# The second input projection's first group multiplies X without its norm, in a float32 kernel of a hybrid layer pair

## The chip, the cores and the metric

The kernel runs on one core of a Trainium2 chip. The time is the device time of one execution in microseconds; the median of three runs is given. The engines are named as in the profile: PE (TensorE), DVE (VectorE), ACT (ScalarE), POOL (GpSimd) and SP (SyncE, which here issues DMAs).

## What is computed

256 tokens of width 2048 pass two layers. The first is attention and a state space scan, then a gated feed-forward of width 5632. The second begins with a norm that is modulated by a vector `c`, and multiplies it by a weight matrix of 7168 columns:

```python
mod = c_act @ w_ada + b_ada
shift, scale, gate = jnp.split(mod, 3, axis=-1)
h = rms_norm_2(x, g) * (1.0 + scale[:, None]) + shift[:, None]
proj = jnp.einsum('bsd,df->bsf', h, w_in)
q_a, k_a, v_a, z_a, q_r, k_r, v_r, z_r = jnp.split(proj, IN_SPLIT_IDX, axis=-1)
```

with `rms_norm_2(x, g) = x * rsqrt(mean(x * x) + 1e-6) * g`. Attention and retention over these, gated by silu of `z_a` and `z_r`, an output projection, the residual and a last norm follow. All is float32. Since the root of the norm is one number per token, `h @ w_in` is also `r * ((x * g * (1 + scale)) @ w_in) + shift @ w_in`.

## The kernel before

X is held transposed: 16 tiles of 128 features x 256 tokens. Each weight matrix comes as a stream of units of 128 x 1024 (two 128-row tiles of 512 columns each). SP loads a unit to one of eight `raw` slots. ACT rounds it to `whi` (line 326, `split`), DVE puts the rest in `wlo` (line 692, `split`); both have four slots. An activation tile is held as `gh` and `gl` in the same way. PE multiplies each unit by three products, hi x hi, hi x lo, lo x hi: 24 matmuls of 256 columns. Eight units make a group of 512 output features, in two PSUM banks; groups use banks 0 and 1, and 2 and 3, in turn. ACT's split of unit n waits until PE has used unit n - 4; DVE's waits for ACT's. Each engine's program is written out in order, with semaphores between them; nothing is reordered.

At the border, the last block of the feed-forward (`B_IN2 - 1`) is eight units. Its last two (`last_pair`, lines 1400 to 1404) finish the last four X tiles one at a time in banks 4 to 7 (`own`); DVE adds them to X (`last_add`, line 1172). ACT squares X in chunks of four tiles (`squares`, lines 341 and 345), DVE sums the squares, and PE reduces them to a column (`column_squares`, line 1421). ACT takes the root (line 361), DVE its reciprocal (line 1200), and PE spreads it over 128 partitions (line 1433). Then, for each of the 16 tiles t:

```python
TH = X[t] * modT[16 + t] * spread        # DVE, line 1206
gh[t] = round(TH + modT[t])              # ACT, line 612
gl[t] = (TH + modT[t]) - gh[t]           # DVE, line 1211
```

`modT` holds shift in columns 0 to 15 and gain x (1 + scale) in 16 to 31. Both loops carry a split behind the tiles 3, 5, 7, ... 15 (`TURNS`). PE's slots n (`stream_in`, n counts the units of this projection) wait in group 0 for each tile's `gl` (`ready`). Group 0 (columns of `z_a`, QB tiles 0 to 3) starts with `product_high_first` (line 1364). ACT copies a finished group to `QB` (line 656). `idle` (line 1455) is a matmul whose result nobody reads. POOL only issues DMAs, the last at 1035.49 us.

## Time and profile before

| | us |
|---|---|
| median of 3 runs (1539.02 to 1539.16) | 1539.11 |
| the profiled execution | 1538.62 |
| its span, first to last instruction | 1536.9 |
| PE busy | 1527.4 (99%) |
| DVE busy | 1135.7 (74%) |
| ACT busy | 780.8 (51%) |
| POOL busy | 27.3 (2%) |

The mean granted clock of PE is 0.999. A busy PE can still be slow, since overlapping matmuls count as busy whatever their spacing. So the distance between the starts of matmuls is to be read beside the busy share. Times below are from the span's start.

### The profile page before, as it was taken

Reading aid. Unit: us, or ns where it says so; the run is one execution under the profiler, and the core shown is the slowest. Engines: PE = TensorE matmul, PEld = TensorE weight load, DVE = VectorE, ACT = ScalarE, POOL = GpSimd, SP = SyncE. Lnnn points to the kernel's source line nnn. Section 1 sums busy time; section 2 is a strip of 40 time slices with the busy share of each in tenths; the row PEclk is TensorE's granted clock in tenths of the full one; section 3 lists DMA queues with packets and bytes.
Section 4 is the critical chain, followed back from the end, with each engine's and each line's share of the span. In section 5 each row is a group of like instructions: output and inputs, shape, how many; then the busy total and the mean of one; then the engine's idle time right before and its main releaser. Section 6 shows DMA issues by size and latency. Waiting matters only on the chain. (4 is left out here: it accounts for less than half of the span.)

```text
span 1536.9 us, 32122 instructions
## 1 busy us (share of the span) xinstructions
PE 1527.4 (99%) x12610; PEld 1486.9 (97%) x12610; DVE 1135.7 (74%) x1371; ACT 780.8 (51%) x933; POOL 27.3 (2%) x55
## 2 busy tenths in 40 slices
PE   9999999999999999999999999999999999999998
PEld 8999997999999999999999999999999989999998
DVE  7877777657987878788788887879854644764754
ACT  7545455545554444444444444445554643454554
POOL 0000000000000000000000000000000000000000
PEclk9999999999999999999999999999999999999999
DMA  9574556457877767677686776866475555445451
GB/s 352 169 272 165 193 178 219 150 166 274 306 281 249 286 233 273 244 251 273 235 292 230 263 272 221 300 220 216 151 247 193 197 192 161 162 157 187 153 184 62
DMA packets 86029, 339.25 MB, mean 221 GB/s; under 512 B 9648, under 2 KB 9920, under 8 KB 79424
## 3 DMA queue, kind: packets, MB, share of 16 engines
q1 hardware_dynamic: 77856, 281.05, 52.8%
q0 software_dynamic: 7232, 54.55, 10.0%
q10 hardware_dynamic: 864, 2.53, 0.4%
q8 instruction: 59, 0.97, 0.2%
q14 instruction: 18, 0.15, 0.0%
HBM read 335.97 MB, written 2.12 MB: 220 GB/s over the span
## 5 line engine op out<-in xcount | busy, mean ns | idle before, releaser
L692 DVE TENSOR_TENSOR wlo<-raw,whi 128x1024 fp32r<-128x1024 f32 x528 | 643.3, 1223 | 346.7 <-ACT whi L326 343.0
L326 ACT ACTIVATE whi<-raw 128x1024 fp32r<-128x1024 f32 x528 | 557.6, 1059 | 647.5 <-PE PS L1333 574.6
L1329 PE MATMUL PS<-gh,whi 128*128 128x256 f32 x3096 | 864.0, 279 | 0.4 <-DVE gl L1211 0.3
L1331 PE MATMUL PS<-gl,whi 128*128 128x256 f32 x3096 | 856.5, 277 | 0.0
L1333 PE MATMUL PS<-gh,wlo 128*128 128x256 f32 x3096 | 856.5, 277 | 0.0
L1329 PEld LDWEIGHTS PS<-gh,whi 128*128 128x128 f32 x3096 | 582.0, 188 | 5.3 <-issue 2.6
L1331 PEld LDWEIGHTS PS<-gl,whi 128*128 128x128 f32 x3096 | 581.7, 188 | 0.8
L1333 PEld LDWEIGHTS PS<-gh,wlo 128*128 128x128 f32 x3096 | 581.5, 188 | 0.0
L1329 PE MATMUL PS<-ah,whi 128*128 128x256 f32 x688 | 189.9, 276 | 0.0
L1331 PE MATMUL PS<-al,whi 128*128 128x256 f32 x688 | 189.9, 276 | 0.0
L1333 PE MATMUL PS<-ah,wlo 128*128 128x256 f32 x688 | 189.9, 276 | 0.0
L1331 PEld LDWEIGHTS PS<-al,whi 128*128 128x128 f32 x688 | 129.2, 188 | 0.0
L1333 PEld LDWEIGHTS PS<-ah,wlo 128*128 128x128 f32 x688 | 129.2, 188 | 0.0
L1329 PEld LDWEIGHTS PS<-ah,whi 128*128 128x128 f32 x688 | 129.1, 188 | 0.0
L1117 DVE SCALAR_TENSOR_TENSOR ada_w<-ada_w,c_act 128x2048 f32<-128x2048 f32 x40 | 91.4, 2285 | 0.0
L1375 PE MATMUL PS<-whi,gh 128*128 128x512 f32 x192 | 76.8, 400 | 0.0
L1378 PE MATMUL PS<-wlo,gh 128*128 128x512 f32 x192 | 75.5, 393 | 0.0
L1377 PE MATMUL PS<-whi,gl 128*128 128x512 f32 x192 | 75.3, 392 | 0.0
L708 DVE TENSOR_TENSOR X<-PS,X 128x1024 f32<-128x1024 f32 x47 | 57.2, 1218 | 0.0
L1375 PEld LDWEIGHTS PS<-whi,gh 128*128 128x128 f32 x192 | 36.1, 188 | 8.6 <-issue 0.8
L1377 PEld LDWEIGHTS PS<-whi,gl 128*128 128x128 f32 x192 | 36.1, 188 | 7.8
L1378 PEld LDWEIGHTS PS<-wlo,gh 128*128 128x128 f32 x192 | 36.1, 188 | 7.5
(259 smaller groups left out, 899.6 us busy)
## 6 DMA issues: line engine op xcount, KB each, us to landing
raw<-weights SPq DMA_DIRECT2D x528, 512.0 KB, 3.6
ada_w<-w_ada POOLq DMA_DIRECT2D x48, 1024.0 KB, 6.4
...
```

Of the source, the lines that this page charges most:

```text
L326: act.activation(whi[:, j % SPLIT, :], raw[:, j, :], ACT.Copy).then_inc(s_hi, 1)
L692: dve.tensor_tensor(wlo[:, j % SPLIT, :], raw[:, j, :], whi[:, j % SPLIT, :].bitcast(F32), ALU.subtract).then_inc(s_lo, 1)
L708: dve.tensor_tensor(x, acc_tiles(par), x, ALU.add).then_inc(s_evac, 1)
L1117: dve.scalar_tensor_tensor(w, w, 1.0, c_act[:, :], ALU.mult, ALU.mult, accum_out=modT[:, bass.ds(i * ADA_STEP + (ADA_FIRST - ADA_STEP + k) ...
L1329: pe.matmul(out[:, t, :], whi[:, b, w], hi[:, kt, :], start=first and half == 0 and (apart or t % 2 == 0), stop=False, skip_group_check=True)
L1331: pe.matmul(out[:, t, :], whi[:, b, w], lo[:, kt, :], start=False, stop=False, skip_group_check=True)
L1333: mm = pe.matmul(out[:, t, :], wlo[:, b, w], hi[:, kt, :], start=False, stop=last and half == 1, skip_group_check=True)
L1375: pe.matmul(out, gh[:, kt, m], whi[:, b, w], start=first and half == 0, stop=False, skip_group_check=True)
L1377: pe.matmul(out, gl[:, kt, m], whi[:, b, w], start=False, stop=False, skip_group_check=True)
L1378: mm = pe.matmul(out, gh[:, kt, m], wlo[:, b, w], start=False, stop=last and half == 1, skip_group_check=True)
```

## The change

Group 0 of the second input projection no longer waits for the norm. ACT and DVE form `YH` and `YL`, the two parts of X x gain x (1 + scale), with no root. Each has two more columns in which the shift stands, so that one matmul of 258 columns gives both products. Group 0 goes to banks 4, 5, 6 and 3, one output tile each (`deferred`). The squares of chunks 1 and 2 are added on POOL, those of the last four tiles (`NEAR`) on DVE. PE sums them over partitions in one matmul in slot 1, into bank 0. ACT takes the root of 256 columns in slot 2, DVE the reciprocal in slot 3 (`rb`). In slot 7 DVE evacuates group 0 times `rb`, and copies the shift's column to `zbias`, which becomes the bias of the silu in slot 16.

`TH`, `gh` and `gl` for the groups from 1 on are made in slots 3 to 14, by the table `TURNED_IN`, which says how many tiles a slot makes. ACT and DVE now split one unit in every slot, with units 2 and 3 ahead of slot 0. `idle` in slot 6, the column form of this root and its spreading are gone.

```diff
+TURNED_IN = (0, 0, 0, 2, 1, 2, 1, 2, 1, 2, 1, 2, 1, 1)
...
+        deferred = (PS[:, 4, 0:S + 2], PS[:, 5, 0:S + 2], PS[:, 6, 0:S + 2], PS[:, 3, 0:S + 2])
+        zbias = small[:, 234:238]
+        def turns(n):
+            done = [sum(TURNED_IN[:m + 1]) for m in range(len(TURNED_IN))]
+            return range(done[n] - TURNED_IN[n], done[n]) if n < len(TURNED_IN) else range(0)
...
+            for c in (1, 2):
+                pool.wait_ge(s_sq, SQUARES[2] + c + 1)
+                if c > 1:
+                    pool.wait_ge(s_sum, SUMS[2] + 1)
+                pool.tensor_tensor(SQX2[:, 0, :, :], SQX2[:, 0, :, :], SQX2[:, 1, :, :], ALU.add).then_inc(s_sum, 1)
+            pool.wait_ge(s_sum, SUMS[2] + 2)
+            pool.tensor_tensor(SQX2[:, 0, 0:2, :], SQX2[:, 0, 0:2, :], SQX2[:, 0, 2:4, :], ALU.add).then_inc(s_far, 1)
+            pool.wait_ge(s_far, 1)
+            pool.tensor_tensor(SQX2[:, 0, 0, :], SQX2[:, 0, 0, :], SQX2[:, 0, 1, :], ALU.add).then_inc(s_far, 1)
...
+            def unscaled_hi(first, end):
+                for t in range(first, end):
+                    act.activation(YH[:, t, 0:S], X[:, t, :], ACT.Copy, scale=modT[:, 16 + t:17 + t]).then_inc(s_yh, 1)
+            def turned_hi(t):
+                act.wait_ge(s_h, t + 1)
+                act.activation(gh[:, t, :], TH[:, t % 8, :], ACT.Identity, bias=modT[:, t:t + 1]).then_inc(s_gh, 1)
+            act.wait_ge(s_mt, 2)
+            act.activation(YH[:, :, S:S + 2], modT[:, 0:DT].unsqueeze(2).to_broadcast([P, DT, 2]), ACT.Copy).then_inc(s_yh, 1)
             for d in range(4):
                 if d < 2:
                     split(B_IN2 - 1, LEAD + 2 * d)
...
                 if d < 3:
                     act.wait_ge(s_evac, G_IN2 - 4 + d + 3)
                 squares(2, d, SQX2)
-                if d == 2:
-                    act.activation(small[:, 241:242], col("eps"), ACT.Sqrt).then_inc(s_warm, 1)
-            column_root(2)
-            for t in range(DT):
-                act.wait_ge(s_h, t + 1)
-                act.activation(gh[:, t, :], TH[:, t % 8, :], ACT.Identity, bias=modT[:, t:t + 1]).then_inc(s_gh, 1)
-                if t in TURNS:
-                    split(B_IN2 - 1, LEAD + 6 + TURNS.index(t))
-            act.dma_start(c2[:, :, :, :], const2).then_inc(s_c2, 16)
+                if d < 3:
+                    unscaled_hi(4 * d, 4 * d + 4)
+            split(B_IN2 - 1, LEAD + 6)
+            split(B_IN2 - 1, LEAD + 7)
+            unscaled_hi(12, DT)
...
             def slot2(n):
...
+                if n == 2:
+                    root(2, D)
+                for t in turns(n):
+                    turned_hi(t)
+                if n == len(TURNED_IN):
+                    act.dma_start(c2[:, :, :, :], const2).then_inc(s_c2, 16)
+                if n == 16:
+                    act.wait_ge(s_zb, 2)
+                    for t in range(4):
+                        ins = act.activation(QB[:, ZA2 + t, :], QB[:, ZA2 + t, :], ACT.Silu, bias=zbias[:, t:t + 1])
+                    ins.then_inc(s_zs, 1)
+                if n == 17:
+                    gate_silu(QB, ZA2 + 4, G_IN2 + 2 + 2, s_zs)
...
-                    split(B_IN2, LEAD + n)
-                if n % 8 == 7:
+                split(B_IN2, LEAD + n)
+                if n % 8 == 7 and n > 7:
                     g = n // 8
                     act.wait_ge(s_used, 8 * B_IN2 + n + 1 + SPLIT)
+                    if g == 1:
+                        act.wait_ge(s_evac, G_IN2 + 3)
                     act.activation(QB[:, 4 * g:4 * g + 4, :], acc_tiles((G_IN2 + g) % 2), ACT.Copy).then_inc(s_evac, 1)
...
+            def unscaled_lo(first, end):
...
                 add_to_x(8 * (B_IN2 - 1) + 2 * d + 1, G_IN2 - 4 + d, (G_IN2 - 4 + d) % 2, 4 * d)
+                if d == 0:
+                    dve.wait_ge(s_yh, 1)
+                    dve.wait_ge(s_mt, 2)
+                    dve.tensor_tensor(YL[:, :, S:S + 2], modT[:, 0:DT].unsqueeze(2).to_broadcast([P, DT, 2]),
+                                      YH[:, :, S:S + 2].bitcast(F32), ALU.subtract).then_inc(s_yl, 1)
             split(B_IN2 - 1, LEAD + 4)
-            sum_chunk(2, 1, SQX2)
+            unscaled_lo(0, 4)
             add_to_x(8 * (B_IN2 - 1) + 5, G_IN2 - 2, (G_IN2 - 2) % 2, 8)
-            fold(2, 1, SQX2)
             last_add(0)
-            dve.wait_ge(s_sq, SQUARES[2] + 3)
-            link(dve.tensor_tensor(SQX2[:, 1, 0:2, :], SQX2[:, 1, 0:2, :], SQX2[:, 1, 2:4, :], ALU.add))
+            split(B_IN2 - 1, LEAD + 5)
             last_add(1)
-            dve.tensor_tensor(SQX2[:, 1, 0, :], SQX2[:, 1, 0, :], SQX2[:, 1, 1, :], ALU.add).then_inc(s_dve, 1)
-            links[0] += 1
+            unscaled_lo(4, 5)
             last_add(2)
-            dve.wait_ge(s_dve, links[0])
-            dve.wait_ge(s_fold, 3)
-            dve.tensor_tensor(SQX2[:, 0, 0, :], SQX2[:, 0, 0, :], SQX2[:, 1, 0, :], ALU.add).then_inc(s_near, 1)
-            near(2, 0, SQX2, 1)
+            unscaled_lo(5, 6)
             last_add(3)
             dve.wait_ge(s_tile, 4)
             dve.sem_inc(s_evac, 1)
-            split(B_IN2 - 1, LEAD + 5)
-            dve.wait_ge(s_mt, 1)
-            dve.wait_ge(s_rcol, 1)
-            dve.reciprocal(rcol[:, 0, :], rcol[:, 0, :]).then_inc(s_icol, 1)
-            dve.wait_ge(s_spread, 1)
-            for t in range(DT + 1):
-                if t < DT:
-                    if t >= 8:
-                        dve.wait_ge(s_gl, 2 * DT + 10 + t - 7)
-                    dve.scalar_tensor_tensor(TH[:, t % 8, :], X[:, t, :], modT[:, 16 + t:17 + t], spread(2),
-                                             ALU.mult, ALU.mult).then_inc(s_h, 1)
-                if t:
-                    k = t - 1
-                    dve.wait_ge(s_gh, 2 * DT + 6 + k + 1)
-                    dve.scalar_tensor_tensor(gl[:, k, :], TH[:, k % 8, :], modT[:, k:k + 1], gh[:, k, :].bitcast(F32),
-                                             ALU.add, ALU.subtract).then_inc(s_gl, 1)
-                    if k in TURNS:
-                        split(B_IN2 - 1, LEAD + 6 + TURNS.index(k))
+            dve.wait_ge(s_sq, SQUARES[2] + 7)
+            link(dve.tensor_tensor(NEAR[:, 0:2, :], NEAR[:, 0:2, :], NEAR[:, 2:4, :], ALU.add))
+            link(dve.tensor_tensor(NEAR[:, 0, :], NEAR[:, 0, :], NEAR[:, 1, :], ALU.add))
+            dve.wait_ge(s_far, 2)
+            dve.tensor_tensor(SQX2[:, 0, 0, :], SQX2[:, 0, 0, :], NEAR[:, 0, :], ALU.add).then_inc(s_fold, 1)
+            split(B_IN2 - 1, LEAD + 6)
+            unscaled_lo(6, 8)
+            split(B_IN2 - 1, LEAD + 7)
+            def turned_tile(t):
+                if t >= 8:
+                    dve.wait_ge(s_gl, 2 * DT + 10 + t - 7)
+                dve.scalar_tensor_tensor(TH[:, t % 8, :], X[:, t, :], modT[:, 16 + t:17 + t], rb[:, :],
+                                         ALU.mult, ALU.mult).then_inc(s_h, 1)
+            def turned_lo(t):
+                dve.wait_ge(s_gh, 2 * DT + 6 + t + 1)
+                dve.scalar_tensor_tensor(gl[:, t, :], TH[:, t % 8, :], modT[:, t:t + 1], gh[:, t, :].bitcast(F32),
+                                         ALU.add, ALU.subtract).then_inc(s_gl, 1)
+            def turned_slot(n):
+                if n < 3:
+                    unscaled_lo((8, 10, 13)[n], (10, 13, 16)[n])
+                if n == 3:
+                    inverse_root(2)
+                    dve.wait_ge(s_rb, 3)
+                for t in turns(n):
+                    turned_tile(t)
+                    if t:
+                        turned_lo(t - 1)
+                if n == len(TURNED_IN):
+                    turned_lo(DT - 1)
+                if n == 7:
+                    finished(8 * B_IN2 + 7, G_IN2)
+                    gates = PS[:, 4:7, :]
+                    dve.tensor_tensor(QB[:, ZA2:ZA2 + 3, :], gates[:, :, 0:S], rb[:, :].unsqueeze(1).to_broadcast([P, 3, S]),
+                                      ALU.mult).then_inc(s_zb, 1)
+                    dve.tensor_copy(zbias[:, 0:3], gates[:, :, S])
+                    dve.tensor_copy(zbias[:, 3:4], deferred[3][:, S:S + 1])
+                    dve.tensor_tensor(QB[:, ZA2 + 3, :], deferred[3][:, 0:S], rb[:, :], ALU.mult).then_inc(s_zb, 1)
+                    dve.wait_ge(s_zb, 2)
+                    dve.sem_inc(s_evac, 1)
...
             for n in range(IN2_SLOTS):
-                if n >= len(TURNS) - 2:
-                    split(B_IN2, LEAD + n)
+                split(B_IN2, LEAD + n)
+                turned_slot(n)
                 slot2(n)
...
+            def product_deferred(b, u):
+                for kt in (2 * u, 2 * u + 1):
+                    pe.wait_ge(s_yl, kt + 2)
+                    for t in range(4):
+                        if u == 0 and kt == 0 and t < 3:
+                            pe.wait_ge(s_tile, t + 1)
+                        w = slice(512 * (kt % 2) + P * t, 512 * (kt % 2) + P * t + P)
+                        hi, lo = YH[:, kt, 0:S + 2], YL[:, kt, 0:S + 2]
+                        pe.matmul(deferred[t], whi[:, b, w], hi, start=(kt == 0), stop=False, skip_group_check=True)
+                        pe.matmul(deferred[t], whi[:, b, w], lo, start=False, stop=False, skip_group_check=True)
+                        mm = pe.matmul(deferred[t], wlo[:, b, w], hi, start=False, stop=(kt == DT - 1), skip_group_check=True)
                 mm.then_inc(s_used, 1)
...
-                if blk == B_IN2 and n == 0:
-                    product_high_first(acc_tiles(grp % 2), need)
+                if blk == B_IN2 and g == 0:
+                    product_deferred(n % SPLIT, u)
                     return
+                if blk == B_IN2 and n == 8:
+                    pe.wait_ge(s_root, 3)
                 product(n % SPLIT, acc_tiles((grp + g) % 2), (2 * u, 2 * u + 1), u == 0, u == 7, gh, gl,
-                        ready=need if g == 0 else None)
+                        ready=need if g == (1 if blk == B_IN2 else 0) else None)
...
-            column_squares(2, SQX2)
 
 
             def slot2(n):
-                if n == 6:
-                    idle(2)
+                if n == 1:
+                    sum_squares(2, SQX2)
```

ACT, from the root of the second layer's norm on, where `whi<-raw` is a split and `gh<-TH` a tile. Before:

```order
L361 ACTIVATE small<-PS,prm 128x2 [waits s_ss]
L612 ACTIVATE gh<-TH,modT 128x256 [waits s_h] x4
L326 ACTIVATE whi<-raw 128x1024 [waits s_used,s_raw2]
L612 ACTIVATE gh<-TH,modT 128x256 [waits s_h] x2
L326 ACTIVATE whi<-raw 128x1024 [waits s_used,s_raw3]
L612 ACTIVATE gh<-TH,modT 128x256 [waits s_h] x2
L326 ACTIVATE whi<-raw 128x1024 [waits s_used,s_raw4]
L612 ACTIVATE gh<-TH,modT 128x256 [waits s_h] x2
```

After:

```order
L344 ACTIVATE whi<-raw 128x1024 [waits s_used,s_raw6]
L372 ACT_TABLE_LOAD
L372 ACTIVATE rb<-PS,prm 128x256 [waits s_ss]
L344 ACTIVATE whi<-raw 128x1024 [waits s_used,s_raw7]
L621 ACTIVATE gh<-TH,modT 128x256 [waits s_h] x2
L344 ACTIVATE whi<-raw 128x1024 [waits s_used,s_raw0]
L621 ACTIVATE gh<-TH,modT 128x256 [waits s_h]
L344 ACTIVATE whi<-raw 128x1024 [waits s_used,s_raw1]
L621 ACTIVATE gh<-TH,modT 128x256 [waits s_h] x2
L344 ACTIVATE whi<-raw 128x1024 [waits s_used,s_raw2]
L621 ACTIVATE gh<-TH,modT 128x256 [waits s_h]
```

The splits stood behind two tiles each; now every slot begins with a split, with two tiles or one behind it.

DVE around the fold of the squares, in the changed kernel:

```order
L1241 TENSOR_TENSOR NEAR<-NEAR 128x512 [waits s_tile,s_sq]
L1242 TENSOR_TENSOR NEAR<-NEAR 128x256 [waits s_dve]
L1244 TENSOR_TENSOR SQX_85<-SQX_85,NEAR 128x256 [waits s_far,s_dve]
L728 TENSOR_TENSOR wlo<-raw,whi 128x1024 [waits s_hi]
L1208 SCALAR_TENSOR_TENSOR YL<-X,modT,YH 128x256 [waits s_yh] x2
L728 TENSOR_TENSOR wlo<-raw,whi 128x1024 [waits s_hi] x2
L1208 SCALAR_TENSOR_TENSOR YL<-X,modT,YH 128x256 [waits s_yh] x2
L728 TENSOR_TENSOR wlo<-raw,whi 128x1024 [waits s_hi]
L1208 SCALAR_TENSOR_TENSOR YL<-X,modT,YH 128x256 [waits s_yh] x3
L728 TENSOR_TENSOR wlo<-raw,whi 128x1024 [waits s_hi]
L1208 SCALAR_TENSOR_TENSOR YL<-X,modT,YH 128x256 [waits s_yh] x3
```

Six splits and ten `YL` tiles stand between the fold (the third row here) and the reciprocal. In the kernel before, DVE in group 0 ran `TH` and `gl` in turn, with a split behind two of each:

```order
L692 TENSOR_TENSOR wlo<-raw,whi 128x1024 [waits s_hi]
L1206 SCALAR_TENSOR_TENSOR TH<-X,modT,PS 128x256
L1211 SCALAR_TENSOR_TENSOR gl<-TH,modT,gh 128x256 [waits s_gh]
L1206 SCALAR_TENSOR_TENSOR TH<-X,modT,PS 128x256
L1211 SCALAR_TENSOR_TENSOR gl<-TH,modT,gh 128x256 [waits s_gh]
L692 TENSOR_TENSOR wlo<-raw,whi 128x1024 [waits s_hi]
L1206 SCALAR_TENSOR_TENSOR TH<-X,modT,PS 128x256
L1211 SCALAR_TENSOR_TENSOR gl<-TH,modT,gh 128x256 [waits s_gh]
```

DVE in slots 3 to 5 now:

```order
L728 TENSOR_TENSOR wlo<-raw,whi 128x1024 [waits s_hi]
L776 RECIPROCAL rb<-rb 128x256 [waits s_root]
L1253 SCALAR_TENSOR_TENSOR TH<-X,modT,rb 128x256 [waits s_rb]
L1253 SCALAR_TENSOR_TENSOR TH<-X,modT,rb 128x256
L1259 SCALAR_TENSOR_TENSOR gl<-TH,modT,gh 128x256 [waits s_gh]
L728 TENSOR_TENSOR wlo<-raw,whi 128x1024 [waits s_hi]
L1253 SCALAR_TENSOR_TENSOR TH<-X,modT,rb 128x256
L1259 SCALAR_TENSOR_TENSOR gl<-TH,modT,gh 128x256 [waits s_gh]
L728 TENSOR_TENSOR wlo<-raw,whi 128x1024 [waits s_hi]
L1253 SCALAR_TENSOR_TENSOR TH<-X,modT,rb 128x256
L1259 SCALAR_TENSOR_TENSOR gl<-TH,modT,gh 128x256 [waits s_gh]
L1253 SCALAR_TENSOR_TENSOR TH<-X,modT,rb 128x256
```

The reciprocal stands behind slot 3's split, and slots of two tiles and of one follow each other.

## Rows read from the trace of the kernel before

**Rows 1.** The page: busy time by engine; costliest groups (busy us, mean ns).
```profile
PE 1527.4 (99%) x12610; PEld 1486.9 (97%) x12610; DVE 1135.7 (74%) x1371; ACT 780.8 (51%) x933; POOL 27.3 (2%) x55
...
L692 DVE TENSOR_TENSOR wlo<-raw,whi 128x1024 fp32r<-128x1024 f32 x528 | 643.3, 1223 | 346.7 <-ACT whi L326 343.0
```

**Rows 2.** PE in order of time at the border (start us, us, line, operands, idle before).
```profile
1095.28 0.28 PE L1404 MATMUL PS<-ah,wlo 128*128 128x256 f32 x1
1095.39 1.02 PE L1421 MATMUL PS<-cst,CG 128*128 128x1 f32 x8
...
1098.26 0.71 PE L1433 MATMUL PS<-cst,small 128*128 128x128 f32 x4 [0.62 <-DVE small L1200]
1098.80 1.03 PE L1455 MATMUL PS<-cst 128*128 128x256 f32 x4
1100.17 0.36 PE L1364 MATMUL PS<-gh,whi 128*128 128x256 f32 x1 [0.34 <-ACT gh L612]
```

**Rows 3.** PE in order of time in groups 0 and 1.
```profile
1108.56 0.36 PE L1329 MATMUL PS<-gh,whi 128*128 128x256 f32 x1
...
1111.70 0.36 PE L1329 MATMUL PS<-gh,whi 128*128 128x256 f32 x1 [0.16 <-DVE gl L1211]
...
1120.81 1.02 PE L1455 MATMUL PS<-cst 128*128 128x256 f32 x4
...
1124.40 0.28 PE L1329 MATMUL PS<-gh,whi 128*128 128x256 f32 x1
...
1146.16 0.28 PE L1329 MATMUL PS<-gh,whi 128*128 128x256 f32 x1
```

**Rows 4.** DVE in order of time in group 0.
```profile
1099.01 0.87 DVE L1206 SCALAR_TENSOR_TENSOR TH<-X,modT,PS 128x256 f32<-128x256 f32 x2 [0.80 <-PE PS L1433]
...
1106.40 1.23 DVE L692 TENSOR_TENSOR wlo<-raw,whi 128x1024 fp32r<-128x1024 f32 x1 [0.35 <-ACT whi L326]
1107.55 0.47 DVE L1206 SCALAR_TENSOR_TENSOR TH<-X,modT,PS 128x256 f32<-128x256 f32 x1
1107.94 0.48 DVE L1211 SCALAR_TENSOR_TENSOR gl<-TH,modT,gh 128x256 fp32r<-128x256 f32 x1
...
1109.55 1.22 DVE L692 TENSOR_TENSOR wlo<-raw,whi 128x1024 fp32r<-128x1024 f32 x1 [0.34 <-ACT whi L326]
...
1111.08 0.48 DVE L1211 SCALAR_TENSOR_TENSOR gl<-TH,modT,gh 128x256 fp32r<-128x256 f32 x1
```

**Rows 5.** ACT in order of time, ahead of the border and in group 0.
```profile
1082.82 1.06 ACT L341 ACTIVATE SQX<-X 128x1024 f32<-128x1024 f32 x1 [2.43 <-DVE X L708]
1083.78 2.05 ACT L326 ACTIVATE whi<-raw 128x1024 fp32r<-128x1024 f32 x2
...
1093.20 1.28 ACT L607 ACT_TABLE_LOAD   x1
...
1105.33 1.05 ACT L326 ACTIVATE whi<-raw 128x1024 fp32r<-128x1024 f32 x1
...
1108.05 0.51 ACT L612 ACTIVATE gh<-TH,modT 128x256 fp32r<-128x256 f32 x1 [1.29 <-DVE TH L1206]
1108.47 1.04 ACT L326 ACTIVATE whi<-raw 128x1024 fp32r<-128x1024 f32 x1
```

**Rows 6.** DVE in order of time at the border: small adds.
```profile
1093.06 0.42 DVE L1172 TENSOR_TENSOR X<-PS,X 128x256 f32<-128x256 f32 x1
1093.39 0.68 DVE L1184 TENSOR_TENSOR SQX<-SQX 128x512 f32<-128x512 f32 x1
```

**Rows 7.** Groups of DVE by line and shape: the reciprocal of the root.
```profile
L739 DVE RECIPROCAL rb<-rb 128x256 f32<-128x256 f32 x2 | 3.5, 1750 | 0.6 <-ACT rb L356 0.6
```

**Rows 8.** Busy us of each engine in two stretches, then granted clock (PEclk).
```profile
1095.00:1101.00 6.00, 4.87 (x36) 4.27 (x36) 4.58 (x11) 2.26 (x8) 0.00 (x0) 1.00 0.27 89
1530.00:1537.00 7.00, 1.37 (x13) 1.13 (x11) 1.50 (x2) 1.72 (x3) 0.00 (x0) 0.77 0.80 300
```

**Rows 9.** Groups of POOL, the costliest (busy us, mean ns, idle before).
```profile
L308 POOL DMA_DIRECT2D ada_w<-w_ada x46 | 24.4, 530 | 757.1 <-DVE ada_w L1117 591.9 <-DVE ada_w L1026 165.3
```

More of the change, by code:

```diff
@@ L670, in _ @@
             column_root(3)
[L671 removed]
+            act.wait_ge(s_icol, 1)
             for b in range(4):
@@ L1492, in sum_squares @@
                     pe.wait_ge(s_root, k)
-                pe.matmul(PS[:, 4, 0:S], ones, buf[:, 0, 0, :], start=True, stop=True).then_inc(s_ss, 1)
+                pe.matmul(PS[:, 0 if k == 2 else 4, 0:S], ones, buf[:, 0, 0, :], start=True, stop=True).then_inc(s_ss, 1)
             pe.wait_ge(s_zero, 1)
```

83 lines of the change are left out of this document (32 added, 51 removed).

## The prediction

> **What bounds the kernel now.** First the page: TensorE (PE) is busy 1527.4 of 1536.9 us [rows 1], so only its holes and the spacing of its matmuls can be changed. Then PE in order of time around the border from the first block to the second. Matmuls follow each other every 0.1133 us, 24 of them a unit (one 1024-column piece of weights), 2.72 us. At 1095.39 that stops: column sums, a wait for the root's reciprocal at 1098.26, two idle matmuls, and the first product of the second input projection only at 1100.17 [rows 2], 4.78 us later. Inside group 0 the units come too slowly: one at 1108.56, the next at 1111.70 with a wait for gl, 3.14 us on, and an idle pair of matmuls stands at 1120.81 [rows 3]; group 0 ends at 1124.40 instead of 1100.17 + 8 x 2.72 = 1121.93, 2.47 us. So the border costs 4.78 + 2.47 = 7.25 us over bare products, and group 1 runs from 1124.40 to 1146.16, 21.76 us, without any loss [rows 3].
>
> Third, who sets the pace inside group 0. VectorE (DVE) and ScalarE (ACT) go in a ring: DVE's low half of a weight piece at 1106.40, tile TH at 1107.55, ACT's gh of it at 1108.05, ACT's next high half whi at 1108.47, DVE's next low half at 1109.55 [rows 4, 5]. That is 3.15 us round (3.14 in the other rounds), for two X tiles a round, against PE's 2.72. This ring is what the change spreads out, and where I look.
>
> **The change part by part.** *Removed.* The 4.78 us hole goes: group 0 multiplies YH and YL, which need no root. Group 0 also loses its ring waits and idle pair, 2.47 us. Added on PE: 192 matmuls of 258 instead of 256 columns (192 x 0.1133 x 2/256 = 0.17 us); one sum of squares of the same form as an idle matmul (about half of the 1.03 us of two [rows 2], 0.5 us); and a wait for X tiles 13 and 14 in the first unit. DVE adds them at about 1095.3 and 1096.1, with 0.42 us each [rows 6], since a split and a YL stand between; PE loses some 0.5 us. If PE were all, the sum would be -7.25 + 1.17 = -6.1 us.
>
> *What runs before the root is known.* Up to ACT's first square at 1082.82 [rows 5] nothing moves. Issue spacings from the rows: ACT 0.97 for a 1024-column piece (1082.82 to 1083.78 [rows 5]) and 0.42 for a 256-column tile (1108.05 to 1108.47 [rows 5]); DVE 1.14 for a split and 0.395 for a tile (1106.40 to 1107.55 to 1107.94 [rows 4]). ACT now puts four YH tiles behind each square: 1082.82 + 0.97 + 4 x 0.42 = 1085.4 for the split that came at 1083.78. DVE follows: splits at 1086.5 and 1087.7, add of chunk 1 at 1088.8, done 1090.05. ACT then: second square 1090.07, four YH, split at 1092.7; the third square waits for DVE's add of chunk 2 (behind a split and four YL, done 1093.9): 1093.93, four YH, four squares of the last chunk, done 1098.3. DVE adds these up (0.71 and 0.47), adds POOL's part, and the fold is issued at 1099.53. PE wants it at about 1101.5, after unit 1, so PE is not held here. But DVE stood about 1.1 us idle and has a backlog behind it.
>
> *The backlog.* From 1099.95 DVE issues six splits, ten YL tiles and the reciprocal of 256 columns (1.75 us [rows 7]): 6 x 1.14 + 10 x 0.395 + 1.78 = 12.57 us. Its inputs come in time (ACT's root with its table load, 1.28 us [rows 5], ends about 1107.8). The first TH tile starts at 1112.5, where before it was 1099.01 [rows 4]. That by itself is no loss: PE needs the first gl only at unit 8, some 1118.3.
>
> *The ring again, now the decisive term.* From slot 3 on, ACT does in each slot: whi of unit n+4, then gh of **all** the TH tiles of that slot; DVE does the low half, then TH, gl. So ACT's next whi waits for the slot's last TH. A slot of one tile is the round of before: 1.15 + 0.50 + 0.42 + 1.08 = 3.15 us. A slot of two adds one TH and one gl ahead of the second TH: 3.15 + 2 x 0.395 = 3.94 us. The table gives slots 4 to 13 one, two, one, two, one, two, one, two, one, one: six of 3.15 and four of 3.94 = 34.7 us, where PE would use 27.2. In slot 7 DVE also turns group 0 out (768 + 256 columns of PSUM and two copies, some 1.5 us; 0.27 of it not covered by the wait for ACT).
>
> Sum: TH of tile 0 at 1112.52; two TH, ACT's gh, then whi of slot 4 at 1113.86; + 34.7 + 0.3 = whi of slot 14 at 1148.9; + 1.09 (ACT's half) + 1.14 (DVE's half) + 0.48 (gl of tile 15) + 0.14 (to PE, as 1111.08 + 0.48 to 1111.70 [rows 3, 4]) = 1151.7. This gl stands in slot 14 behind a split that waits for unit 14, and PE needs it for the second half of unit 15, 1.36 us and a restart of 0.09: group 1 ends at **1153.1**. Before, it ended at 1146.16 [rows 3]. So +6.9 us: PE arrives at unit 8 about 6 us earlier and then loses some 12 us in front of the halves of units 10 to 15. What is late next: nothing; from unit 16 on the weights are four units ahead, and a unit of PE covers a split on ACT and DVE again (1.05 and 1.22 us [rows 4, 5]). The four silu of 256 instead of one of 1024, some 0.7 us more on ACT, lie under that.
>
> *POOL.* Two adds of 1024, one of 512 and one of 256 columns go to POOL, which shows no arithmetic in this trace, only DMA issues of 0.53 us [rows 9]. Bounds: as on DVE (1.22 [rows 1], 0.68 and 0.42 [rows 6]), or four times that, the ratio of DVE's slowest 256-column step to an add (1.75 to 0.42 [rows 6, 7]). Cover: POOL has from 1095.1 (third square) to 1099.5, 4.4 us, for 1.22 + 0.68 + 0.42 = 2.32 us of adds at DVE's pace, so up to 1.9 times it costs nothing; above that each microsecond goes one to one into the fold, then the backlog and the end (at four times +7). I take two and a half times, the middle: 2.5 x 2.32 = 5.8, with the third square 0.4 late, +1.8 us.
>
> Forecast: 1538.62 (the profiled execution) + 6.9 + 1.8 = 1547.3; the median of before is 0.49 above it, so **1547.8 us**.
>
> **A rule against the change.** No row of before has POOL and DVE adding at once. The Trainium skill (SBUF — State Buffer, Who interferes with whom) says that a VectorE instruction with two SBUF inputs contends with a GpSimd one that reads SBUF, and that the second to issue blocks fully until the first ends; no run here shows it. GPSIMD Engine Reference (Elementwise — side-by-side cycle accounting) has a GpSimd add at 1.96 times the VectorE's; by that price POOL would still be all but covered, and the forecast would be near 1546.2.
>
> **Rivals.**
> *The ports (35%).* DVE's splits and YL tiles have both inputs in SBUF. If a POOL add holds them up whole, the two large ones (2 x 3.05 us at my price) fall among DVE's work between 1091 and 1099.5, of which 1.1 us is idle: +5 on DVE, all of it ahead of the ring. 1552.8; with POOL as fast as DVE about 1549. This mechanism is the rule above.
> *Faster (4%).* The ring does not close: ACT issues the next whi without standing behind the slot's gh, so that a slot takes what DVE is busy, 1.14 + 0.79 or 1.14 + 1.58 us. DVE then catches up with PE after its late start at 1112.5, and only the gl of tiles 14 and 15, which stand behind splits that wait for units 13 and 14, hold PE, 1.8 us together. Group 1 ends at 1118.3 + 21.76 + 1.8 = 1141.8, 4.3 us early: 1534.8. The point from which it decides is the mean of the ten rounds: at 2.8 us the end is that of before (1113.9 + 28 + 2.85 + 1.4 = 1146.2), at my 3.5 it is 7 us later. For it: DVE's own work is short enough. Against it: the 3.15 us round of rows 4 and 5, in which ACT and DVE idle in turn, by order of issue, and the order listed in the change.
> *Nothing to measure (5%).* The mean round is 2.6 to 3.0 us: 1539.
>
> *The clock (4%).* PE will stand about 12 of 28 us. If the granted clock (1.00 with 4.87 of 6 us busy, 0.77 with 1.37 of 7 [rows 8]) falls to its lower level, 1.2 GHz, units take 5.44 us, longer than the ring's 3.5: six units x 1.9 = 11 more, 1559.
> *The change does not do what it says*, since group 0 waits for YL instead: YL comes at 0.395 a tile against 1.36 us of PE each, with a split per two; in the ports' case it can happen, and is in its price.
>
> **How the numbers follow.** Forecast case 51%, between 1546.0 (POOL covered) and 1553 (four times DVE's time). The ports 35%, clock 4%, faster 4%, nothing 5%, 1% unnamed. The range 1545.0 to 1553.5 takes the forecast case and most of the ports' and leaves under 2 in 10 out. A measurement of this kernel tells about 0.2%, 3.1 us, from no change; slower than that has 0.51 + 0.35 + 0.04 = 0.90 (with the unnamed 0.91), same 0.05, faster 0.04.
>
> **What the changed profile would show.** Right: products of 258 columns directly behind 1095.39 with gaps under 1 us in the first unit; the next unit 8 near 1118 to 1122; DVE's low halves spaced 3.15 and 3.94 us in turn from 1115 to 1149, with DVE idle for ACT and ACT idle for DVE; PE waiting for gl in both halves of units 10 to 15, 1.1 to 1.8 us each; then no waits. Wrong: spacing of 2.72 us there; DVE's splits or YL stretched beyond 1.22 and 0.48 us while POOL adds (ports); POOL's 1024 columns beyond 5 us; a granted clock under 0.95 between 1120 and 1155.

## The result

The changed kernel took 1555.28 us, median of four executions, beside 1539.13 us of the kernel before on the same chip: ratio 1.0098, 95% interval 1.0086 to 1.011. The forecast was 1547.8 with a range of 1545.0 to 1553.5, so the sign was right and the size outside the range. The four executions are 1555.53, 1555.03, 1556.04 and 1550.87. The lone one at 1550.87 matters: five more executions of the same kernel on another chip, told below, lie between 1550.69 and 1552.02. Two causes have to be kept apart: about 12 us that every execution has, and 4.3 us more in three of those first four. Five executions of three kernels below took some 26 us longer than the others of the same kernel (1561.71 to 1570.27), and they are left out of every median and ratio.

The profiled execution is the one of 1555.53 (span 1553.8). Its trace runs later than that of before even ahead of the border: a split of ACT there, released by PE in both, starts at 1080.20 instead of 1079.33. Against before, its times are therefore read less 0.9 us.

### The profile page after: what moved, and what is told of

Same layout as the page of the kernel before. It is cut to its first block, busy times and chain, and to the rows that moved or that the text cites. A ratio compares the mean times of both kernels' runs of the same rounds, so it can differ in the third digit from the quotient of the medians.

```text
span 1553.8 us, 32123 instructions
## 1 busy us (share of the span) xinstructions
PE 1533.3 (99%) x12584; PEld 1492.0 (96%) x12584; DVE 1146.4 (74%) x1388; ACT 787.0 (51%) x951; POOL 34.5 (2%) x59
## 4 chain that ended last, share of the span: by engine, by line
PE 91%; DVE 5%; ACT 2%; issue 1%; ACTq 0%; DVEq 0%
PE PS L1399 26%; PE PS L1401 26%; PE PS L1403 26%; PE PS L1447 3%; PE PS L1445 3%; PE PS L1448 3%; DVE wlo L728 2%; ACT whi L344 1%; PE PS L1601 1%; PE PS L1622 1%; DVE conv_acc L804 1%; PE PS L1790 0%; PE PS L1584 0%; DVE YL L1208 0%; DVE TH L1253 0%
## 5 line engine op out<-in xcount | busy, mean ns | idle before, releaser
L1399 PE MATMUL PS<-gh,whi 128*128 128x256 f32 x3040 | 850.1, 280 | 9.4 <-DVE gl L1259 9.4
L1401 PE MATMUL PS<-gl,whi 128*128 128x256 f32 x3040 | 842.6, 277 | 0.0
L1403 PE MATMUL PS<-gh,wlo 128*128 128x256 f32 x3040 | 842.5, 277 | 0.0
L1399 PEld LDWEIGHTS PS<-gh,whi 128*128 128x128 f32 x3040 | 571.6, 188 | 14.9 <-DVE gl L1259 6.2
L1403 PEld LDWEIGHTS PS<-gh,wlo 128*128 128x128 f32 x3040 | 572.0, 188 | 0.0
L1401 PEld LDWEIGHTS PS<-gl,whi 128*128 128x128 f32 x3040 | 571.1, 188 | 0.8
```

The lines of the kernel that those rows point to most:

```text
L1399: pe.matmul(out[:, t, :], whi[:, b, w], hi[:, kt, :], start=first and half == 0 and (apart or t % 2 == 0), stop=False, skip_group_check=True)
L1401: pe.matmul(out[:, t, :], whi[:, b, w], lo[:, kt, :], start=False, stop=False, skip_group_check=True)
L1403: mm = pe.matmul(out[:, t, :], wlo[:, b, w], hi[:, kt, :], start=False, stop=last and half == 1, skip_group_check=True)
```

## The profile after

The page, with the same rows as [rows 1] of before. PE's busy time rose by 5.9 us though it stands longer in front of `gl`, so its matmuls follow each other more slowly somewhere.

```profile
PE 1533.3 (99%) x12584; PEld 1492.0 (96%) x12584; DVE 1146.4 (74%) x1388; ACT 787.0 (51%) x951; POOL 34.5 (2%) x59
...
L728 DVE TENSOR_TENSOR wlo<-raw,whi 128x1024 fp32r<-128x1024 f32 x528 | 643.1, 1222 | 353.5 <-ACT whi L344 349.9
```

PE's waits between 1080 and 1180 us (waited for: us in total, times, longest). The column form's waits of [rows 2] are gone; 12.8 us of new ones stand there.

```profile
PE PS L1399 <- DVE gl L1259: 9.4, 8, 1.6
PE PS L1434 <- DVE X L1217: 3.4, 3, 1.8
```

**The ring.** DVE in order of time behind the root (start us, us, line, operands; in brackets the idle time before and who ended it). This answers [rows 4].

```profile
1117.10 1.75 DVE L776 RECIPROCAL rb<-rb 128x256 f32<-128x256 f32 x1
1118.88 0.88 DVE L1253 SCALAR_TENSOR_TENSOR TH<-X,modT,rb 128x256 f32<-128x256 f32 x2
...
1121.29 1.23 DVE L728 TENSOR_TENSOR wlo<-raw,whi 128x1024 fp32r<-128x1024 f32 x1 [0.87 <-ACT whi L344]
1122.44 0.48 DVE L1253 SCALAR_TENSOR_TENSOR TH<-X,modT,rb 128x256 f32<-128x256 f32 x1
1122.83 0.48 DVE L1259 SCALAR_TENSOR_TENSOR gl<-TH,modT,gh 128x256 fp32r<-128x256 f32 x1
1124.44 1.23 DVE L728 TENSOR_TENSOR wlo<-raw,whi 128x1024 fp32r<-128x1024 f32 x1 [1.13 <-ACT whi L344]
...
1128.38 1.23 DVE L728 TENSOR_TENSOR wlo<-raw,whi 128x1024 fp32r<-128x1024 f32 x1 [1.13 <-ACT whi L344]
...
1131.53 1.23 DVE L728 TENSOR_TENSOR wlo<-raw,whi 128x1024 fp32r<-128x1024 f32 x1 [1.13 <-ACT whi L344]
...
1156.30 1.23 DVE L728 TENSOR_TENSOR wlo<-raw,whi 128x1024 fp32r<-128x1024 f32 x1 [1.13 <-ACT whi L344]
```

The splits are 3.15, 3.94 and 3.15 us apart, and so on to 1156.30, with DVE idle 1.13 us for ACT each time. Only slot 7, where DVE also turns group 0 out, is longer, 4.30 us. Those are the forecast's two slots to the hundredth. ACT's side of the same ring, where it stands for DVE's `TH` and takes up the next `whi` only behind it, answers [rows 5]:

```profile
1151.66 0.51 ACT L621 ACTIVATE gh<-TH,modT 128x256 fp32r<-128x256 f32 x1 [1.69 <-DVE TH L1253]
1152.08 1.05 ACT L344 ACTIVATE whi<-raw 128x1024 fp32r<-128x1024 f32 x1
1154.81 0.51 ACT L621 ACTIVATE gh<-TH,modT 128x256 fp32r<-128x256 f32 x1 [1.69 <-DVE TH L1253]
...
1155.22 1.04 ACT L344 ACTIVATE whi<-raw 128x1024 fp32r<-128x1024 f32 x1
```

PE in order of time where the ring holds it: the last four of its eight waits for `gl` (in units 13, 14 and 15, the last in both halves), then the first product of group 2. This answers [rows 3].

```profile
1148.14 0.38 PE L1399 MATMUL PS<-gh,whi 128*128 128x256 f32 x1 [1.43 <-DVE gl L1259]
...
1152.08 0.39 PE L1399 MATMUL PS<-gh,whi 128*128 128x256 f32 x1 [0.95 <-DVE gl L1259]
...
1155.32 0.36 PE L1399 MATMUL PS<-gh,whi 128*128 128x256 f32 x1 [1.59 <-DVE gl L1259]
...
1157.97 0.39 PE L1399 MATMUL PS<-gh,whi 128*128 128x256 f32 x1 [1.03 <-DVE gl L1259]
...
1159.49 0.28 PE L1399 MATMUL PS<-gh,whi 128*128 128x256 f32 x1
```

Less the 0.9 us, group 1 ends at 1158.6, 12.4 us after the 1146.16 of [rows 3]; the forecast had 6.9 without POOL and 8.7 with it.

**POOL and DVE.** POOL in order of time, all its arithmetic, and DVE beside it.

```profile
1092.01 2.61 POOL L323 TENSOR_TENSOR SQX<-SQX 128x1024 f32<-128x1024 f32 x1 [55.10 <-ACT SQX L357]
1098.01 2.50 POOL L323 TENSOR_TENSOR SQX<-SQX 128x1024 f32<-128x1024 f32 x1 [3.39 <-ACT SQX L357]
1100.59 1.33 POOL L325 TENSOR_TENSOR SQX<-SQX 128x512 f32<-128x512 f32 x1
1102.00 0.80 POOL L327 TENSOR_TENSOR SQX<-SQX 128x256 f32<-128x256 f32 x1
```

```profile
1091.87 3.83 DVE L1208 SCALAR_TENSOR_TENSOR YL<-X,modT,YH 128x256 fp32r<-128x256 f32 x4
...
1098.56 2.24 DVE L1208 SCALAR_TENSOR_TENSOR YL<-X,modT,YH 128x256 fp32r<-128x256 f32 x1
1100.72 0.41 DVE L1217 TENSOR_TENSOR X<-PS,X 128x256 f32<-128x256 f32 x1
1101.05 1.15 DVE L1208 SCALAR_TENSOR_TENSOR YL<-X,modT,YH 128x256 fp32r<-128x256 f32 x1
1102.13 0.41 DVE L1217 TENSOR_TENSOR X<-PS,X 128x256 f32<-128x256 f32 x1
```

A `YL` tile takes 0.48 us alone, four 1.67. One that is issued inside a POOL add ends some 0.28 us behind that add: 1098.56 + 2.24 = 1100.80 behind 1098.01 + 2.50 = 1100.51, and 1102.20 behind 1101.92. Held so, the tiles lose 2.16 + 1.76 + 0.67 = 4.6 us. The add of PSUM to X at 1102.13, with one input in SBUF, lies wholly within POOL's last add and takes its usual 0.41. This is the ports rival's mechanism. The Trainium skill (SBUF — State Buffer, Who interferes with whom) has both halves of it: two SBUF inputs contend with a GpSimd instruction that reads SBUF, at most one does not. Here its rule and the trace agree.

POOL's own times are not those of POOL alone: each of its four adds begins while a DVE instruction with two SBUF inputs is still running. What an add takes with nothing beside it, no run shows.

**The clock.** Busy us of PE, PEld, DVE, ACT, POOL in five stretches, then the granted clock; the last of them is after the ring.

```profile
1095.00:1100.00 5.00, 2.74 (x19) 2.06 (x17) 5.00 (x7) 3.13 (x7) 1.99 (x1) 0.91 0.31 62
1100.00:1105.00 5.00, 3.82 (x17) 3.82 (x18) 4.45 (x8) 2.98 (x6) 2.64 (x3) 0.50 0.20 79
...
1120.00:1140.00 20.00, 17.74 (x149) 17.14 (x147) 14.46 (x25) 9.58 (x14) 0.00 (x0) 1.00 0.39 133
1140.00:1160.00 20.00, 12.89 (x101) 11.99 (x102) 12.26 (x21) 8.56 (x13) 0.00 (x0) 1.00 0.55 198
1180.00:1200.00 20.00, 20.00 (x172) 20.00 (x171) 8.58 (x7) 8.55 (x9) 0.00 (x0) 1.00 0.54 186
```

The clock fell to half, the level of 1.2 GHz, in the first unit, where PE stands for X with 2.74 of 5 us busy, and not in the ring, where the clock rival expected it: between 1120 and 1160 it stays 1.00 with 30.6 of 40 us busy. At half clock 20 matmuls stand 0.215 us apart instead of 0.120, 1.9 us. It comes with the waits for X: all five profiled executions with POOL's adds have the fall (0.50 to 0.66 in 1100 to 1105), and the others stay at 1.00.

Most of this is hidden, since PE stands for `gl` later in any case. Not all of it is. ACT's split of a unit waits until PE has used an older one, and DVE's split waits for ACT's, so a late PE also delays the first `TH`:

```profile
1111.98 1.06 ACT L344 ACTIVATE whi<-raw 128x1024 fp32r<-128x1024 f32 x1 [2.25 <-PE PS L1436]
1113.08 1.23 DVE L728 TENSOR_TENSOR wlo<-raw,whi 128x1024 fp32r<-128x1024 f32 x1 [0.89 <-ACT whi L344]
```

DVE is idle 0.89 us here and 0.47 at the next split; without POOL's adds the two are 0.16 together. In the second trace of the changed kernel, told below, the same waits for X bring a shorter fall, with 11 matmuls at half clock:

```profile
1100.00:1105.00 5.00, 4.45 (x25) 4.45 (x26) 4.45 (x8) 3.47 (x7) 2.09 (x2) 0.66 0.11 43
```

There, on before's time, the first `TH` starts 0.6 us earlier (1117.4 against 1118.0), and group 1 ends 0.7 us earlier (1157.9 against 1158.6).

**The spacing.** In the last of these rows the clock is 1.00 and PE busy throughout, yet it holds 172 matmuls, where before has 179. The same window of the kernel before:

```profile
1180.00:1200.00 20.00, 20.00 (x179) 20.00 (x178) 9.38 (x8) 10.37 (x11) 0.00 (x0) 1.00 0.60 200
```

From the last wait at 1157.97 to 1249.94 us each matmul follows the one before by 0.1178 us instead of 0.1133, and nothing waits. The 192 matmuls of 512 columns behind them stand 0.2290 us apart, as before (0.2289); then come 24 more at 0.1178, up to 1296.74. From the end of group 1 to that point this trace takes 137.3 us and the second one 133.7, so the spacing costs 3.5 us. The forecast has no term for it.

The level changed at waits. In this trace the matmuls settle at 0.1133 behind each of the first seven waits of the ring, and at 0.1178 behind the last. In the second trace they run at 0.1178 behind the wait at 1154.03 and at 0.1133 behind the next, at 1156.69. The kernel before has it too: 24 matmuls at 0.1178 behind the wait at 1111.70 of [rows 3].

## The experiments

Eleven runs were made on three chips: nine new kernels, one of them twice, and the changed kernel once more. Before's median was 1539.42 beside the first four, 1539.70 beside the next four and 1539.10 beside the last three, so times of different groups may be compared to about 0.6 us.

**Is it POOL?** POOL's four adds are left out and their signals passed on. The norm then lacks the squares of eight X tiles.

```diff
-                pool.tensor_tensor(SQX2[:, 0, :, :], SQX2[:, 0, :, :], SQX2[:, 1, :, :], ALU.add).then_inc(s_sum, 1)
+                pool.sem_inc(s_sum, 1)
...
+            pool.sem_inc(s_far, 2)
```

> The changed kernel with POOL's four adds left out (the norm then lacks the squares of eight X tiles; POOL only passes the signals on). Theory: of the 16 us that the change costs, some 5.4 come from POOL's adds holding up DVE's tiles, which moves the first TH tile from 1118.0 (aligned to the trace of before) to 1112.6 us, and all of it is handed on by the ring. So: YL tiles back at 0.48 us, PE's wait for X tiles in the first unit down from 3.4 to under 0.6 us, no fall of the granted clock there, time 1549.9 us. Rival: the adds cost nothing that isn't lost in the ring anyway (DVE has slack between the border and slot 3): 1555 us, with the same start of the ring.

Measured 1547.39 (1545.33 to 1549.18), ratio 1.0048 (1.0031 to 1.0065). DVE with no POOL beside it, at the place of the rows above:

```profile
1091.47 1.67 DVE L1203 SCALAR_TENSOR_TENSOR YL<-X,modT,YH 128x256 fp32r<-128x256 f32 x4
...
1095.99 0.47 DVE L1203 SCALAR_TENSOR_TENSOR YL<-X,modT,YH 128x256 fp32r<-128x256 f32 x1
...
1099.41 0.42 DVE L1239 TENSOR_TENSOR SQX<-SQX,NEAR 128x256 f32<-128x256 f32 x1
```

The tiles are back at their length, PE has no wait for X left in the first unit, and its clock stays at 1.00. The first `TH` starts at 1112.1, read on before's time (its trace is 0.46 late), where the forecast without POOL had 1112.5. PE still waits 9.2 us for `gl`, eight times: the ring is independent of POOL. The profiled execution, the one of 1549.18, has 172 matmuls in 1180 to 1200, so it is one at the slow spacing; the two fastest, 1545.33 and 1546.33, are 6.4 us above before. In the profiled one, whose slow stretch begins at the end of group 1, that end comes 6.5 us later than before's, which fits the two. The median is 2.5 us under the theory's 1549.9 and far from the rival's 1555; neither number took the two spacings into account.

**The same adds on DVE.** The ring is kept, and DVE sums the squares by its own adds.

```diff
+            sum_chunk(2, 1, SQX2)
...
+            sum_chunk(2, 2, SQX2)
+            dve.wait_ge(s_sum, SUMS[2] + 2)
+            link(dve.tensor_tensor(SQX2[:, 0, 0:2, :], SQX2[:, 0, 0:2, :], SQX2[:, 0, 2:4, :], ALU.add))
+            link(dve.tensor_tensor(SQX2[:, 0, 0, :], SQX2[:, 0, 0, :], SQX2[:, 0, 1, :], ALU.add))
```

> The changed kernel with POOL's four adds made by DVE instead. Theory: DVE is held for about as long as a POOL add lasts whenever a two-input tile of its own meets it, so that its own adds, 1.14 + 1.14 + 0.7 + 0.4 = 3.4 us of issue, cost less than POOL's four: the ring starts some 3 us earlier than in the changed kernel and the time is 1552 us. Rival: the adds cost more on the engine that is the bound: 1557 us or more.

Measured 1551.93 (1548.66 to 1553.01), ratio 1.0076, as the theory had it. On before's time the first `TH` starts at 1114.9, 3.1 us earlier than in the changed kernel. PE's wait for X falls from 3.4 to 0.8 us; that for `gl` stays, 10.1. The profiled execution, 1551.75, has the slow spacing (173 matmuls in the window); the one of the changed kernel at that spacing took 1555.53. Moving the adds back is worth less than leaving them out, since their time on DVE lies ahead of the ring too.

**Is it the ring?** `TH` goes ahead of the slot's split on DVE, so that ACT finds it ready; the split is followed by `gl` of the same tiles, where before it was `gl` of the tile ahead. In slot 3 the reciprocal goes ahead of the split as well. Nothing else is changed; POOL still adds.

```diff
                 for t in turns(n):
-                    turned_tile(t)
-                    if t:
-                        turned_lo(t - 1)
...
+                    turned_lo(t)
...
+                for t in turns(n):
+                    turned_tile(t)
                 split(B_IN2, LEAD + n)
                 turned_slot(n)
```

> The changed kernel, with DVE making the TH tiles of a slot ahead of the slot's split instead of behind it; the same instructions otherwise. Theory of the ring: ACT's gh no longer waits for DVE's split, slots come back to PE's 2.72 us and group 1 ends 13.4 us earlier: 1542 us if the slow pace of 0.1178 stays, 1538 if it goes with the waits. Rival: DVE's sheer work behind its late start (TH tile 0 at 1118) sets the end; then the end moves by under 4 us, 1551 or more.

Measured 1539.82 (1538.94 to 1545.38, ten executions), ratio 1.0006 (0.9997 to 1.0016): no difference from before. The theory had 1538 or 1542, by the spacing; the rival, 1551 or more, is out. The profiled execution has the fast spacing; the one of 1545.38 may be one at the slow. The waits for `gl` are gone and that for X stays:

```profile
PE PS L1432 <- DVE X L1217: 3.5, 3, 1.9
```

DVE's splits in four slots of it. It stands for ACT by 0.22 us at most, and a slot takes 2.32 to 2.62 us, less than PE's 2.72:

```profile
1120.76 1.22 DVE L728 TENSOR_TENSOR wlo<-raw,whi 128x1024 fp32r<-128x1024 f32 x1
...
1123.09 1.22 DVE L728 TENSOR_TENSOR wlo<-raw,whi 128x1024 fp32r<-128x1024 f32 x1
...
1125.41 1.22 DVE L728 TENSOR_TENSOR wlo<-raw,whi 128x1024 fp32r<-128x1024 f32 x1
...
1128.03 1.23 DVE L728 TENSOR_TENSOR wlo<-raw,whi 128x1024 fp32r<-128x1024 f32 x1 [0.22 <-ACT whi L344]
```

So the order of DVE's instructions within a slot made some 11 us (1539.82 against 1550.97). The clock fell to 0.50 in 1100 to 1105 here as well. With no wait for `gl` left to hide it, the fall now counts: again 20 matmuls at half clock, 1.9 us.

**Both together.** The edits of the two kernels above, the sums on DVE and `TH` ahead of the split.

> Both: TH tiles ahead of the slot's split, and the sums on DVE. Theory: with the ring open, what is left of the loss is the late first unit and the late fold; group 1 ends 3 us ahead of the kernel before: 1536.3 us, or 1541 where the slow pace of 0.1178 us sets in behind a wait. Rival: once the ring is open the sums no longer matter, 1539.8 us as with the tiles ahead alone.

Measured 1535.54, the median of seven, ratio 0.9975 (0.9964 to 0.9986). Six of them lie between 1535.13 and 1536.38; the profiled one, 1540.89, has 172 matmuls in 1180 to 1200. Both groups that the expectation named appear, and the rival, 1539.8, is out. Against its own before the kernel is 4.6 us faster than with `TH` ahead alone. The traces account for 4.2 of them: the wait for X is 2.7 us shorter, the clock's fall of 1.9 us is gone, and 0.4 us of waiting for `wlo` are new. So with the ring open POOL's adds still cost over 4 us, nearly half of it through the clock.

**What sets the spacing?** First on the kernel before, without its idle pair in slot 6:

```diff
-                if n == 6:
-                    idle(2)
```

> The kernel before without its pair of idle matmuls behind unit 6. Theory: the pair sets the pace back to 0.1133 us after the waits of group 0; without it PE may go on at 0.1178 for up to 150 us, and the time is 1543 us, or, where the last wait happens to leave the fast pace, 0.8 us under before, 1538.3, so that its runs fall into two groups. Rival: the pair only fills time, 1538.3 us in every run.

Measured 1543.71, the median of six, ratio 1.0024 (1.0012 to 1.0037). Four stand at 1543.59 to 1544.42, two at 1538.86 and 1539.89. Two more took 1570.27 and 1569.27. The profiled execution is the first of these: it goes over to 0.1178 at 413 us, behind a pause of 0.26 us for which the profile shows no wait, and has 172 matmuls in the window 1180 to 1200. So the spacing of the six was not seen, only their times: two groups, 4.7 us apart. The kernel before itself was never above 1541 in 53 executions beside these experiments; one more took 1566.29, and may be such a one. So this pair of matmuls, whose result nobody reads, seems to be worth some 5 us where it stands, in most executions. Then an idle pair in the changed kernel behind its last wait, in slot 15:

```diff
+                if n == 15:
+                    idle(2)
```

> The changed kernel with one pair of idle matmuls behind unit 15, as stood behind unit 6 before. Theory: after the waits of group 1 PE goes on at 0.1178 us a matmul instead of 0.1133, at a granted clock of 1.00, until the next pair of float32 matmuls some 135 us later; a pair of idle ones ends that at once. Gain about 135 x 0.038 = 5.1 less 0.8 for the pair: 1551.0 us, and spacing of 0.1133 us from unit 16 on. Rival: the slower pace comes from elsewhere (operands, other engines' traffic) and stays: 0.1178 us from unit 16 on and 1556 us.

Measured 1552.43 (1551.99 to 1552.69), with 179 matmuls in the window. Taken with the first result it looks as if the pair set the spacing right. Its trace speaks against it: behind the last wait, at 1157.70, the matmuls begin at 0.118 us and are back at 0.1133 from 1158.4, and the pair comes only at 1159.19. It was then run on one chip beside the changed kernel itself, unchanged, and with the same two lines added to the kernel that has both cures:

> The changed kernel unchanged, beside its twin with an idle pair behind unit 15, to tell how often each is at the slow spacing of matmuls (0.1178 us instead of 0.1133 after the ring). Theory A, the pair behind the last wait prevents the slow spacing: most of these executions lie near 1555.5, a few near 1551.5, and none of the twin's does more than 1 us above 1552.4. Theory B, the spacing is drawn at random in every execution whatever stands there: both kernels show two groups 4 us apart in like shares, here 1551.3 and 1555.5.

> The changed kernel with an idle pair behind unit 15, once more, on the chip of the changed kernel. Theory A: one group, 1551.9 to 1552.8, median 1552.4, 3 below the changed kernel's median. Theory B: two groups, 1552.4 and 1556.5, with the upper one in like share as in the changed kernel.

> The kernel with TH ahead of the split and the squares' sums on VectorE, and an idle pair behind unit 15. Its twin without the pair gave six executions from 1535.1 to 1536.4 and one of 1540.9 at the slow spacing. Theory A, the pair prevents the slow spacing: one group at 1536.15 + 0.6 = 1536.7, none above 1538. Theory B, it prevents nothing: one execution in seven or so near 1541.5.

Measured 1550.97 (1550.69 to 1552.02, five executions) for the changed kernel, 1552.59 (1551.72 to 1553.21, five) with the pair, 1536.88 (1535.78 to 1537.44, eleven) for the third. By its time no execution of any of the three had the slow spacing, so on that chip the pair only cost 1.6 us. The changed kernel there, waits and window:

```profile
PE PS L1399 <- DVE gl L1259: 9.2, 8, 1.6
PE PS L1434 <- DVE X L1217: 3.5, 3, 1.9
```

```profile
1180.00:1200.00 20.00, 20.00 (x179) 20.00 (x178) 8.57 (x7) 9.13 (x9) 0.00 (x0) 1.00 0.60 190
```

The same waits as in the first result, the fast spacing, the shorter fall of the clock, and 4.3 us less. Of nine executions of the changed kernel three have the time of the slow spacing, all on the first chip; of nine with the pair none. Theory A expected most of the changed kernel's executions near 1555.5 there, and theory B two groups in both: neither came. The third kernel came as theory A had it, one group and none above 1538; but by theory B, at one in seven, eleven such executions in a row are a chance of 18%, and the twin without the pair ran on another chip. The pair's help is not shown.

**The better order.** Both cures; DVE's last four X adds ahead of `YL` 2 to 5, with `YL` 1 between them; unit 2's split ahead of the fold; the sum of squares in slot 2; and tiles earlier in the table.

```diff
-TURNED_IN = (0, 0, 0, 2, 1, 2, 1, 2, 1, 2, 1, 2, 1, 1)
+TURNED_IN = (0, 0, 0, 2, 1, 2, 1, 2, 2, 2, 2, 2)
```

> As the run with both edits, and: DVE adds the X tiles 12 to 15 before it makes YL tiles 1 to 5, unit 2's split goes ahead of the fold on ACT and DVE, the sum over partitions goes to slot 2, and the table turns two tiles in each of slots 7 to 11. Theory: PE has no wait in the first unit (before 3.4 us in the changed kernel), the clock does not fall, group 1 ends 5 us ahead of the kernel before: 1534.5 us, 1539 where the slow pace sets in. Rival: the waits only move to unit 2 and 3, 1536.5 us.

Measured 1535.30 (1534.37 to 1536.18, nine executions), ratio 0.9971 (0.9961 to 0.9981): 4.4 us, or 0.3%, faster than before. The theory had 1534.5, the rival 1536.5, and the result lies between: the waits of the first unit are gone, and one of 1.1 us stands in unit 2. Against the kernel with both cures alone (1535.54) the further edits show no gain. The clock holds:

```profile
PE PS L1428 <- DVE wlo L719: 1.1, 1, 1.1
```

```profile
1100.00:1105.00 5.00, 3.91 (x33) 3.71 (x32) 4.83 (x9) 4.28 (x7) 0.00 (x0) 1.00 0.15 42
```

With an idle pair behind unit 5 of it:

```diff
+                if n == 5:
+                    for _ in range(2):
+                        pe.matmul(PS[:, 1, 0:S], ident, cst[:, 16:16 + S], start=True, stop=True)
```

> The same with a pair of idle matmuls behind unit 5. Theory of the pace: all runs at 0.1133 us a matmul from there on, 1535.2 us with a spread under 1 us, where the kernel without the pair falls into two groups. Rival: the pair only costs its 0.8 us in each run.

Measured 1536.07 (1535.34 to 1541.81): three of ten executions at 1540.07, 1541.24 and 1541.81, and the profiled one of them shows 172 matmuls in the window. An idle pair there is no guard, against the expectation.

## Why the prediction was right, and where it failed

**The ring: right.** Slots of 3.15 and 3.94 us, DVE and ACT idle in turn, none of PE's waits behind unit 15. PE's waits in front of `gl` are eight, one of 0.5 and seven of 0.9 to 1.6 us, where the prediction had both halves of six units with 1.1 to 1.8. Without POOL and at the fast spacing the end is 6.4 us later, where the sum had +6.9; and the order that opens the ring takes all of it away. The rival "faster" named what is needed for that, a mean slot under 2.8 us, and the experiment with `TH` ahead got there by changing the order and not by luck.

**POOL: the failed step.** The sum took POOL at 2.5 times DVE's time and nothing else, +1.8 us. Its adds were quicker than that (2.61 and 2.50 us for 1024 columns, where DVE takes 1.22: 2.1 times), so by the sum's own reckoning POOL was almost covered: its last three took 4.6 us, where the sum had 4.4 of cover. But they held DVE's `YL`, for 4.6 us. The held `YL` made the X adds late, PE stood for X, its clock fell, and its late units held up the splits. So the first `TH` came 5.9 us later than without POOL (1118.0 against 1112.1), and 5.3 in the second trace. The changed kernel at 1551.0, against 1545.3 and 1546.3 without POOL's adds, makes 5.5 us of the end, each taken against its own before (+11.9 and +6.4), where the sum had 1.8. The ports rival, at 35%, had +5 for exactly this and gave 1552.8. The choice between the two cases was the error: the place where both engines would add was known from the working, and the tile that DVE would issue there has two SBUF inputs.

**The spacing: the missing term.** 1551.0, the changed kernel with every wait in it, lies in the range; 1555.28 does not. That 1551.0 lies in it is the work of the range, which was drawn to take in the ports rival, and not of the sum. Of the 4.3 us between the two, the traces put 3.5 on matmuls at 0.1178 us and 0.7 on the longer fall of the clock. The warning was at hand: the section on the time before says that busy PE can be slow, and before's own trace has 24 matmuls at 0.1178 behind a wait. The prediction takes the units from 16 on as unchanged ("What is late next: nothing"). That PE's spacing might come out otherwise behind new waits was no rival. The sum thus missed +3.2 (forecast 1547.8, at the fast spacing 1551.0) by POOL, +3.7, less 0.5 that the ring was shorter (6.4 against 6.9), and +4.3 by the spacing and the clock.

**PE's own terms: too small.** 258 columns were taken in proportion, 0.1142 us each. Group 0's matmuls follow each other by 0.1200:

```profile
1112.60 0.28 PE L1434 MATMUL PS<-YH,whi 128*128 128x258 f32 x1
1112.72 0.29 PE L1435 MATMUL PS<-YL,whi 128*128 128x258 f32 x1
1112.84 0.28 PE L1436 MATMUL PS<-YH,wlo 128*128 128x258 f32 x1
1112.96 0.28 PE L1434 MATMUL PS<-YH,whi 128*128 128x258 f32 x1
```

(the changed kernel at the fast spacing). 192 x 0.0067 = 1.3 us, not 0.17. In the changed kernel that hides in the slack before unit 8. In the kernel with both cures it counts: -7.25 + 1.3 + 0.5 + 1.2 (its waits for X and `wlo` in group 0) = -4.3, where the forecast had -6.1 if PE were all, and -4.2 was measured. The wait for X tiles was put at 0.5 us and was 3.4, since the held `YL` stand ahead of the adds. It was hidden in part only: through the splits it moved the first `TH`. Nor did PE come to unit 8 early. On before's time that unit starts at 1125.3 in the first trace and 1124.7 in the second, later than before's 1124.40, where the prediction had 1118.3; without POOL's adds it starts at 1119.4.

**The clock: right in the ring, missed in the first unit.** It fell for some 6 us where PE has slack in the changed kernel, and the rival had it in the ring only. The longer of its two falls cost 0.7 us at the end; the price of 1.9 us shows in full only with the ring open. Of the prediction's signs, unit 8 between 1118 and 1122 did not come. Of its signs of error, the stretched `YL` came, and the granted clock under 0.95 between 1120 and 1155 did not.

## What stays open

What makes a stretch of matmuls run at 0.1178 us. It stands with a granted clock of 1.00, begins behind a wait in the changed kernel (1157.97), but at the first 256-column matmuls, at 1121, in both kernels with `TH` ahead that were traced at it, 17 us behind the last wait in one of them. In these two the matmuls of 512 columns are slow as well, 0.2333 us instead of 0.2289; in the changed kernel they are not. The program doesn't fix it: the changed kernel was traced at either spacing, and several others show, by their times, executions of both kinds. But the program has a share in it: by their times the kernel before kept to the fast spacing 53 times of 54 with its pair in slot 6, and without it two of eight times. It does not follow the fall of the clock: the profiled execution with `TH` ahead has that fall and is fast, the one without POOL has none and is slow. Executions of the changed kernel differ between chips, but the chips were not crossed with enough kernels to say that the chip decides.
